# Sixteen-head attentions with a float32 values' product on column halves of TensorE

## The chip, the cores and the metric

The kernel runs on one NeuronCore of a Trainium2 chip. A core has TensorE (PE, the matrix engine), VectorE (DVE), ScalarE (ACT), GpSimd (POOL) and SyncE (SP, which here only starts loads). Each engine takes its own instructions in order, and semaphores order the engines among themselves. SBUF is the on-chip memory of 128 partitions; PSUM is the memory into which TensorE writes, in 8 banks of 512 float32 values a partition. The metric is the device time in microseconds (us); lower is better.

## The reference, cut to what matters

Two transformer blocks over 256 positions of width 1024, all in float32. The second block has two attentions of 16 heads each. For every head a softmax of scores over 256 keys is multiplied with 64-wide values:

```python
def block_attention(q, k, v, scale):          # 8 + 8 heads: "att2" in the kernel
    sc = jnp.einsum('bkgqd,bksd->bkgqs', qblk, kt).astype(jnp.float32) * scale
    p = jax.nn.softmax(sc, axis=-1).astype(vt.dtype)
    return jnp.einsum('bkgqs,bksd->bkgqd', p, vt)

def neighbourhood_attention(h, w_qkv, rpb, w_out):   # 16 heads: "att3"
    sc = jnp.einsum('bhqd,bhqkd->bhqk', qblk, kg).astype(jnp.float32) * scale + bias[None]
    p = jax.nn.softmax(sc, axis=-1).astype(vg.dtype)
    return jnp.einsum('bhqk,bhqkd->bhqd', p, vg)
```

The rest (a first block with convolutions and a 4-head attention "att1", and three feed-forward layers) is not touched.

## The kernel before, in words

Nearly every product is made in three passes: each operand is split into an upper part in fp32r (a reduced-precision float32 that TensorE multiplies in one pass) and the lower rest, and upper x upper, upper x lower and lower x upper are summed in PSUM. ScalarE makes the upper parts (`..hi`), VectorE or GpSimd the lower ones (`..lo`). The weights come in 1 MB groups through three slots (`raw`, `whi`, `wlo`), and the output projection of an attention is woven into its heads, so that the weights' work hides behind them.

The order of the work is written out by hand: each engine's block of code calls the same steps in its own order. No scheduler and no planner is involved. In att2 and att3 the 16 heads are 8 pairs (`PAIRS`). The steps of a head i of pair u, with the names used from here on:

- S(u), scores: TensorE, `pair_scores` or `scores` (lines 2209 and 2159). They go to PSUM bank 0 (even head) and 1 (odd head). Where a head's queries and keys take 64 partitions (pairs 0 to 3 of att2, all of att3), the products of the two heads stand on the two row halves of the array (64x128); pairs 4 to 7 of att2 take 96 rows and use the whole array.
- maxima: VectorE (line 1290; in att3 line 1283, two instructions a head that also add the bias).
- exp(i), exponentials: ScalarE (line 759), in place in the PSUM bank, with the row sums.
- divided(i): VectorE (lines 1299 and 1303), from that bank into `prob` in SBUF, 3 buffers.
- T(i), transposes of the probabilities: TensorE (line 2221), four 128x128, into the rows' bank. `rows_bank` gives bank 2 to all heads but head 1, which has bank 5 in att2 and bank 4 in att3.
- rows, split: ScalarE copies the bank into the upper part (line 802), VectorE makes the lower part (line 1310) and thereby frees the bank.
- V(i), values' product: TensorE, `head_times_values`, 6 products a head of 128x128 by 256 columns (line 2159, via `parts_product`). The values of a head are 64 wide; the other 64 columns of the left operand are zeros, so that both heads of a pair add up in bank 3. The values are split by GpSimd (`values_of`, lines 511 and 475), the zeros are written by ScalarE (`zeros_beside_values`, line 740).
- output, split: ScalarE (line 785) and VectorE (line 1339), out of bank 3.
- half(u, n): TensorE, half n of the output projection of pair u, 6 products of 512 columns (line 2013).

In round u of the loop in TensorE's `woven_heads` stand, for u of 3 and more: T(2u), V(2u-1), S(u+1), half(u-2, 1), T(2u+1), V(2u), half(u-1, 0). The first pairs of scores and T(0) are issued ahead of the loop. The scores of pair u+1 wait for `at_p`, that is for divided() of pair u, since exponentials and division both use the scores' banks.

## Time and profile before

| | us |
|---|---|
| median of 3 runs (1154.97 to 1155.78) | 1155.02 |
| the profiled execution, its own time | 1157.38 |
| its span | 1155.6 |
| TensorE (PE) busy | 1140.1 (99%) |
| VectorE busy | 839.0 (73%) |
| ScalarE busy | 628.1 (54%) |
| GpSimd busy | 497.3 (43%) |
| the woven heads of att2 in the span | about 621 to 672 |
| the woven heads of att3 in the span | about 921 to 972 |

The span is what the profile's rows cover; the profiled execution's own time also counts what lies around it. Busy time of an engine is the union of its instructions. A matmul's row shows its full duration, from the first column to the last result, while the next one may start long before it ends: the distance between two starts is the cost of a matmul, and the duration is not. The granted TensorE clock is at full speed (the mean is 0.998) throughout.

### The profile page before, as it was taken

What the parts mean: (1) busy time and instruction counts of PE and PEld (TensorE: products, weight loads), DVE (VectorE), ACT (ScalarE), POOL (GpSimd) and SP (SyncE); (2) the same over time, 40 slices, a digit from 0 to 9 for tenths busy, and PEclk for the clock granted to TensorE, in tenths of its full rate; (3) what the DMA queues carried; (4) which work ended last, traced back from release to release, by engine and by line L of the source; (5) the groups of instructions that cost most, each with busy time, mean ns of one, the idle gap of its engine ahead of it and who ended that gap; (6) DMA issues with size and microseconds to landing.
All of it is one profiled execution on the core that took longest, in us unless ns stands there. A gap on an engine that the chain in (4) does not pass through costs nothing.

```text
span 1155.6 us, 18538 instructions
## 1 busy us (share of the span) xinstructions
PE 1140.1 (99%) x6964; PEld 1019.0 (88%) x6964; DVE 839.0 (73%) x1100; ACT 628.1 (54%) x858; POOL 497.3 (43%) x433
## 2 busy tenths in 40 slices
PE   8999999999999999999999999999999999999997
PEld 8999999889998888888897888888888888888886
DVE  4687989886676898777898776665666676656655
ACT  6544433566644666555668755444464677444443
POOL 2699998897200633333233528880010455000000
PEclk9999999999999999999999999999999999999999
DMA  9555555563357456545442287556555513665651
GB/s 301 181 183 184 182 182 182 182 217 110 114 179 221 155 198 198 200 163 195 156 138 106 74 230 252 182 185 207 189 171 194 177 42 120 208 193 192 197 181 37
DMA packets 142809, 201.08 MB, mean 174 GB/s; under 512 B 3300, under 2 KB 123108, under 8 KB 142748
## 3 DMA queue, kind: packets, MB, share of 16 engines
q1 hardware_dynamic: 141776, 196.88, 51.8%
q0 software_dynamic: 912, 3.17, 1.2%
q8 instruction: 39, 0.64, 0.2%
q10 hardware_dynamic: 60, 0.20, 0.1%
q14 instruction: 22, 0.18, 0.0%
HBM read 199.20 MB, written 1.05 MB: 173 GB/s over the span
## 4 chain that ended last, share of the span: by engine, by line
PE 91%; DVE 2%; issue 2%; POOL 2%; ACT 2%; DMA 0%; POOLq 0%; ACTq 0%; DVEq 0%
PE ps L2013 52%; PE ps L2050 21%; PE ps L2055 11%; PE ps L2159 3%; PE ps L2221 1%; POOL wlo L483 1%; PE ps L2209 1%; PE ps L2141 1%; POOL merged L598 0%; DMA x<-in_x 0%; DVE work L1303 0%; PE ps L2127 0%; ACT ps L759 0%; DVE p_parts L1235 0%; PE ps L2427 0%
## 5 line engine op out<-in xcount | busy, mean ns | idle before, releaser
L1208 DVE TENSOR_TENSOR wlo<-raw,whi 128x2048 fp32r<-128x2048 f32 (+1 forms) x162 | 376.7, 2326 | 130.8 <-ACT whi L669 129.8
L669 ACT ACTIVATE whi<-raw 128x2048 fp32r<-128x2048 f32 (+1 forms) x178 | 337.4, 1897 | 140.9 <-PE ps L2013 134.4
L2050 PE MATMUL ps<-p_parts,whi 128*128 128x512 f32 x1184 | 289.3, 391 | 0.0
L2050 PEld LDWEIGHTS ps<-p_parts,whi 128*128 128x128 f32 x1184 | 220.1, 188 | 44.8
L2013 PE MATMUL ps<-p_parts,whi 128*128 128x256 f32 x912 | 166.4, 285 | 0.6 <-DVE p_parts L1235 0.6
L2055 PE MATMUL ps<-p_parts,wlo 128*128 128x256 f32 x1184 | 163.3, 282 | 0.0
L2055 PEld LDWEIGHTS ps<-p_parts,wlo 128*128 128x128 f32 x1184 | 155.8, 191 | 5.5
L2013 PE MATMUL ps<-whi,q_hi 128*128 128x512 f32 x380 | 148.6, 391 | 0.2 <-POOL wlo L483 0.2
L2013 PE MATMUL ps<-whi,q_lo 128*128 128x512 f32 x380 | 148.3, 390 | 0.0
L2013 PE MATMUL ps<-wlo,q_hi 128*128 128x512 f32 x380 | 147.9, 389 | 0.0
L2013 PEld LDWEIGHTS ps<-p_parts,whi 128*128 128x128 f32 x912 | 143.7, 194 | 1.1 <-issue 1.0
L483 POOL TENSOR_TENSOR wlo<-raw,whi 128x512 fp32r<-128x512 f32 x60 | 83.4, 1415 | 108.0 <-ACT whi L669 98.8
L2013 PE MATMUL ps<-p_parts,wlo 128*128 128x256 f32 x456 | 129.7, 284 | 0.0
L573 POOL TENSOR_SCALAR work<-misc,vec 128x256 f32<-128x256 f32 x84 | 125.2, 1490 | 0.0
L469 POOL TENSOR_TENSOR stat<-stat 128x1 f32<-128x1 f32 x14 | 10.0, 745 | 223.7 <-DVE stat L1216 210.6
L876 ACT ACTIVATE work<-ps 128x512 f32<-128x512 f32 x52 | 30.9, 595 | 135.1 <-PE ps L2055 135.0
L577 POOL TENSOR_TENSOR misc<-misc,work 128x256 f32<-128x256 f32 x84 | 91.5, 1090 | 7.0
L2013 PEld LDWEIGHTS ps<-p_parts,wlo 128*128 128x128 f32 x456 | 88.3, 194 | 0.0
L2013 PEld LDWEIGHTS ps<-wlo,q_hi 128*128 128x128 f32 x380 | 71.4, 188 | 15.2
L2013 PEld LDWEIGHTS ps<-whi,q_hi 128*128 128x128 f32 x380 | 71.5, 188 | 14.3 <-issue 0.5
L2013 PEld LDWEIGHTS ps<-whi,q_lo 128*128 128x128 f32 x380 | 71.5, 188 | 13.2
L491 POOL TENSOR_TENSOR wlo<-raw,whi 128x2048 fp32r<-128x2048 f32 x5 | 23.6, 4725 | 101.9 <-ACT whi L669 101.9
(320 smaller groups left out, 1835.6 us busy)
## 6 DMA issues: line engine op xcount, KB each, us to landing
raw<-in_w_in SPq DMA_DIRECT2D x35, 1024.0 KB, 5.0
raw<-in_w_up SPq DMA_DIRECT2D x22, 1024.0 KB, 5.1
raw<-in_up_a SPq DMA_DIRECT2D x16, 1024.0 KB, 5.4
raw<-in_down_a SPq DMA_DIRECT2D x16, 1024.0 KB, 4.9
raw<-in_up_b SPq DMA_DIRECT2D x16, 1024.0 KB, 5.4
raw<-in_down_b SPq DMA_DIRECT2D x16, 1024.0 KB, 4.9
raw<-in_od_w_qkv SPq DMA_DIRECT2D x12, 1024.0 KB, 5.1
raw<-in_w_down SPq DMA_DIRECT2D x11, 1024.0 KB, 5.0
```

The costliest lines, as they stand in the source:

```text
L483: last = nc.gpsimd.tensor_tensor(out=wlo[:, g % R, part], in0=raw[:, g % R, part], in1=whi[:, g % R, part].bitcast(F32), op=ALU.subtract)
L491: nc.gpsimd.tensor_tensor(out=wlo[:, g % R, :], in0=raw[:, g % R, :], in1=whi[:, g % R, :].bitcast(F32), op=ALU.subtract).then_inc(lo_read ...
L573: nc.gpsimd.tensor_scalar(tap, src, w, None, ALU.mult).then_inc(pool_mul, 1)
L577: nc.gpsimd.tensor_tensor(out=dst, in0=dst, in1=tap, op=ALU.add).then_inc(pool_tap, 1)
L669: nc.scalar.activation(whi[:, g % R, 0:n], raw[:, g % R, 0:n], ACT.Copy).then_inc(hi_ready, 1)
L876: return nc.scalar.activation(dst.rearrange("p (h n) -> p h n", h=2), ps[:, 2 * pb:2 * pb + 2, S:BW], ACT.Copy)
L1208: nc.vector.tensor_tensor(wlo[:, g % R, 0:n], raw[:, g % R, 0:n], whi[:, g % R, 0:n].bitcast(F32), ALU.subtract).then_inc(lo_ready[g % R], 1)
L2013: ins = nc.tensor.matmul(dst, lhs, rhs, start=first and n == 0, stop=last and n == 2)
L2050: return nc.tensor.matmul(bank(2 * pb + h), whi[:, r, at], p_parts[:, :, S * k:S * k + S], start=k == 0, stop=False)
L2055: return nc.tensor.matmul(bank(2 * pb + h, 0, S), wlo[:, r, at], p_hi[:, S * k:S * k + S], start=False, stop=k == KD - 1)
L2141: last = nc.tensor.transpose(bank(low + c // 2, c % 2 * S + P * t, c % 2 * S + P * t + P), x[:, t, P * c:P * c + P], ident[:, :])
L2159: ins = nc.tensor.matmul(dst, a, b, start=first and n == 0, stop=last and n == 2)
```

## The change

The change concerns att2 and att3; of att1 only the place of its maxima in `stat` moves.

1. The values' product is one float32 product with the unsplit operands: for each pair 2 heads x 2 halves of the keys, 4 matmuls of 128x64 by 256 columns. The even head's result is written to partitions 0 to 63 and the odd one's to 64 to 127 of bank 3, so the left operands stand on the two column halves of the array (the built program has tile size 128x64 for them). The zeros beside the values, the split of the values on GpSimd, and the split of the transposed rows are gone. A transposed row block is copied out once, into one of four SBUF buffers (`turned_rows`): by ScalarE for even heads, by VectorE for odd ones.
2. Exponentials are written to four SBUF buffers (`exp_rows`); in att3 the biased scores go there as well. A score bank is therefore free once the exponentials are done (att2) or once the maxima with the bias are done (att3), and the division reads SBUF.
3. Scores run two pairs ahead instead of one: in round u the order on TensorE is T(2u), V of pair u-1, T(2u+1), S(u+2), half(u-2, 1), half(u-1, 0). ScalarE's and VectorE's loops are written in a matching new order.

```diff
+        turned_rows = [misc[:, 1024 + 512 * n:1536 + 512 * n] for n in range(4)]
+        exp_rows = [a.rearrange("p (t n) -> p t n", t=T) for a in (work[:, 0:512], work[:, 2048:2560],
+                                                                   misc[:, 3072:3584], misc[:, 3584:4096])]
...
             def exponentials(name, i):
                 units, H, u0, n0, biased, k = ATT[name]
                 act.wait_ge(at_nm, n0 + i + 1)
+                if name != "att1" and i >= 4:
+                    act.wait_ge(at_p, n0 + i - 3)
                 for t in range(T):
                     scored = bank(S_BANK[name] + i % 2, t * S, t * S + S)
-                    src = bsc[:, i % 2, t, :] if biased else scored
-                    last = nc.scalar.activation(scored, src, ACT.Exp,
-                                                bias=att_nmax[:, 2 * (i % 2) + t:2 * (i % 2) + t + 1],
+                    dst = scored if name == "att1" else exp_rows[i % 4][:, t, :]
+                    last = nc.scalar.activation(dst, dst if biased else scored, ACT.Exp,
+                                                bias=att_nmax[:, 2 * (i % 4) + t:2 * (i % 4) + t + 1],
...
-                def rows_upper(i):
+                def rows_out(i):
                     act.wait_ge(at_t, n0 + i + 1)
-                    if i >= 2:
-                        act.wait_ge(at_v, n0 + i - 1)
-                    nc.scalar.activation(unit_hi[i % 2][:, PT], bank(rows_bank(name, i)[0]), ACT.Copy).then_inc(at_h, 1)
+                    if i >= 4:
+                        act.wait_ge(at_v, n0 + i - 3)
+                    b = rows_bank(name, i)[0]
+                    nc.scalar.activation(turned_rows[i % 4], bank(b), ACT.Copy).then_inc(bank_read[b], 1)
...
-                    if u == 1:
-                        rows_upper(2 * u + 1)
-                    if u + 1 < PAIRS and u:
-                        exponentials(name, 2 * u + 2)
-                    if u != 1:
-                        rows_upper(2 * u + 1)
-                    if u + 1 < PAIRS and u:
-                        exponentials(name, 2 * u + 3)
...
                         queries_keys(name, u + 3)
+                    if u + 2 < PAIRS:
+                        exponentials(name, 2 * u + 4)
+                        exponentials(name, 2 * u + 5)
...
-                nc.vector.tensor_tensor(prob[:, i % 3], ps[:, S_BANK[name] + i % 2, :].rearrange("p (t n) -> p t n", t=T),
-                                        inv.to_broadcast([P, T, S]), ALU.mult).then_inc(at_p, 1)
+                rows = ps[:, S_BANK[name] + i % 2, :].rearrange("p (t n) -> p t n", t=T) if name == "att1" else exp_rows[i % 4]
+                nc.vector.tensor_tensor(prob[:, i % 3], rows, inv.to_broadcast([P, T, S]), ALU.mult).then_inc(at_p, 1)
...
+                    rows_out(2 * u + 1)
+                    if u:
+                        output_lower(u - 1)
+                    if u + 2 < PAIRS:
+                        maxima(name, 2 * u + 4)
+                        maxima(name, 2 * u + 5)
...
                 if u:
-                    pe.wait_ge(at_p, n0 + 2 * u)
+                    pe.wait_ge(at_nm if biased else at_e, n0 + 2 * u)
...
+                def pair_times_values(u):
...
+                    for i in (2 * u, 2 * u + 1):
+                        b, uses = rows_bank(name, i)
+                        free(b, uses + 1)
                     free(3, USES[name][3] + u)
                     for m in range(2):
-                        v0, p0 = UNIT_V + S * m + HD * h, UNIT + S * m
-                        ins = parts_product(bank(3, 0, S), [a[:, v0:v0 + P] for a in unit_sides(u, H)],
-                                            [a[i % 2][:, p0:p0 + S] for a in (unit_hi, unit_lo)],
-                                            h == 0 and m == 0, h == 1 and m == 1)
-                    ins.then_inc(at_v, 1)
+                        for h in range(2):
+                            rows = turned_rows[(2 * u + h) % 4]
+                            ins = nc.tensor.matmul(ps[HD * h:HD * h + HD, 3, 0:S], units[u]["v"][:, m, h, :], rows[:, S * m:S * m + S],
+                                                   start=m == 0, stop=m == 1)
+                            if m == 1:
+                                ins.then_inc(at_v, 1)
...
                 for u in range(PAIRS + 1):
...
+                    if 0 < u < PAIRS:
                         rows_transposed(name, 2 * u, *rows_bank(name, 2 * u))
...
+                    if u:
+                        pair_times_values(u - 1)
                     if u < PAIRS:
                         rows_transposed(name, 2 * u + 1, *rows_bank(name, 2 * u + 1))
-                        head_times_values(2 * u)
+                    if u + 2 < PAIRS:
+                        pair_scores(name, u + 2)
+                    if u > 1:
+                        half_of_output(u - 2, 1)
                     if u:
                         half_of_output(u - 1, 0)
```

How the order changes is shown at three places; the line numbers of the changed kernel differ from those of the one before. First TensorE in att2 of the kernel before, from T(1) on (`x3` counts equal instructions in a row, the brackets name the semaphores waited for; L2221 transposes, L2159 values' product, L2209 scores):

```order
L2221 MATMUL ps<-ident,work 128x128 [waits at_p,bank_read5]
L2221 MATMUL ps<-ident,work 128x128 x3
L2159 MATMUL ps<-q_hi 128x256 [waits bank_read2,bank_read3,v_lo,v_zero]
...
L2221 MATMUL ps<-ident,work 128x128 [waits at_p,bank_read2]
L2221 MATMUL ps<-ident,work 128x128 x3
L2159 MATMUL ps<-p_parts,q_hi 128x256 [waits bank_read3,bank_read5,v_lo]
...
L2209 MATMUL ps<-p_parts,q_hi 128x256 [waits at_p,qk_lo]
...
L2221 MATMUL ps<-ident,work 128x128 [waits at_p,bank_read2]
L2221 MATMUL ps<-ident,work 128x128 x3
```

The same place of TensorE in the changed kernel (L2178 transposes, L2218 values' product, L2166 scores):

```order
L2178 MATMUL ps<-ident,work 128x128 [waits at_p,bank_read5]
L2178 MATMUL ps<-ident,work 128x128 x3
L2166 MATMUL ps<-p_parts,q_hi 128x256 [waits at_e,qk_lo]
...
L2178 MATMUL ps<-ident,work 128x128 [waits at_p,bank_read2]
L2178 MATMUL ps<-ident,work 128x128 x3
L2218 MATMUL ps<-misc,gates 64x256 [waits bank_read5,bank_read2,bank_read3,bank_read7]
L2218 MATMUL ps<-misc,gates 64x256 x3
L2178 MATMUL ps<-ident,work 128x128 [waits at_p,bank_read2]
L2178 MATMUL ps<-ident,work 128x128 x3
L2166 MATMUL ps<-p_parts 128x256 [waits at_e,qk_lo]
```

S(2) now stands ahead of T(2) and of every values' product, V(0) and V(1) are one block behind T(2), and S(3) follows T(3) directly; S waits for exponentials (`at_e`) instead of a division (`at_p`).

ScalarE in att2 of the changed kernel, from the exponentials of heads 2 and 3 on (L728 exponentials, L716 half of a weight group's upper part, L695 queries or keys, L774 rows copied out, L754 output):

```order
L728 ACTIVATE misc,stat<-ps,stat 128x256 [waits at_nm]
L728 ACTIVATE misc,stat<-ps,stat 128x256
L716 ACTIVATE whi<-raw 128x1024 [waits slot_used,raw_in2]
L695 ACTIVATE p_parts<-merged 128x256 [waits at_s,bank_read6]
L728 ACTIVATE work,stat<-ps,stat 128x256 [waits at_p,at_nm]
L728 ACTIVATE work,stat<-ps,stat 128x256
L728 ACTIVATE work,stat<-ps,stat 128x256 [waits at_p,at_nm]
L728 ACTIVATE work,stat<-ps,stat 128x256
L774 ACTIVATE misc<-ps 128x512 [waits at_t]
L754 ACTIVATE o_up<-ps 128x256 [waits at_v]
```

And of the kernel before, from the same exponentials on (L759 exponentials, L802 rows' upper part, L722 queries or keys, L749 weights, L785 output):

```order
L759 ACTIVATE ps,stat<-ps,stat 128x256 [waits at_nm]
L759 ACTIVATE ps,stat<-ps,stat 128x256
L802 ACTIVATE p_parts<-ps 128x512 [waits at_t]
L722 ACTIVATE q_hi<-merged 128x256 [waits at_s,at_q]
L749 ACTIVATE whi<-raw 128x1024 [waits slot_used,raw_in2]
L722 ACTIVATE p_parts<-merged 128x256 [waits at_s,bank_read6]
L802 ACTIVATE q_hi<-ps 128x512 [waits at_v,at_t]
L785 ACTIVATE o_up<-ps 128x256 [waits at_v]
```

The copy of the rows of head 2 (L774 now, L802 in the last but one row before) stood ahead of the exponentials of heads 4 and 5 and now stands behind them.

VectorE in att2 of the changed kernel, from the division of head 2 on (L1260 divided, L1305 copies of keys, L1320 rows of head 1 copied out, L1246 maxima of heads 4 and 5):

```order
L1260 TENSOR_TENSOR work<-misc,stat 128x512 [waits at_rs]
L1305 COPY vreg<-ps 96x512 [waits ev_tr]
L1255 RECIPROCAL stat<-stat 128x2 [waits at_e]
L1260 TENSOR_TENSOR work<-misc,stat 128x512 [waits at_t,at_rs]
L1305 COPY vreg<-ps 96x512 [waits ev_tr] x2
L1320 COPY misc<-ps 128x512 [waits at_t]
L1246 TENSOR_REDUCE stat<-ps 128x2 [waits at_s] x2
```

Before, the lower part of the rows of head 1 (L1310) stood ahead of the division of head 3:

```order
L1303 TENSOR_TENSOR work<-ps,stat 128x512 [waits at_rs]
L1354 COPY vreg<-ps 96x512 [waits ev_tr]
L1310 TENSOR_TENSOR p_parts<-ps,p_parts 128x512 [waits at_h]
L1299 RECIPROCAL stat<-stat 128x2 [waits at_e]
L1303 TENSOR_TENSOR work<-ps,stat 128x512 [waits at_t,at_rs]
L1354 COPY vreg<-ps 96x512 [waits ev_tr] x2
```

The rows of head 1, which the first values' product needs, now come behind one division and two more copies.

## Rows read from the trace of the kernel before

**Rows 1.** Windows: from:to, length, then busy us and instructions of each engine.

```profile
616.50:625.00 8.50, 7.75 (x68) 7.02 (x68) 8.43 (x14) 8.28 (x22) 1.46 (x2) 1.00 0.37 125
625.00:638.00 13.00, 11.43 (x82) 9.75 (x81) 9.07 (x20) 10.66 (x29) 9.03 (x8) 1.00 0.13 35
...
921.50:937.00 15.50, 14.35 (x111) 12.15 (x111) 10.99 (x33) 12.65 (x35) 7.47 (x13) 1.00 0.22 67
937.00:972.00 35.00, 35.00 (x234) 29.56 (x230) 24.36 (x70) 25.01 (x66) 24.41 (x26) 1.00 0.20 65
```

**Rows 2.** Waits of TensorE: line waited for, total us, times, longest.

```profile
PE ps L2221 <- DVE p_parts L1310: 1.6, 2, 0.8
```

**Rows 3.** Timeline of TensorE, end of att2: start, us, engine, line, what.

```profile
661.80 0.60 PE L2221 MATMUL ps<-ident,work 128*128 128x128 f32 x4
662.15 0.48 PE L2159 MATMUL ps<-p_parts,q_hi 128*128 128x256 f32 x2
662.47 0.28 PE L2159 MATMUL ps<-p_parts,q_lo 128*128 128x256 f32 x1
...
666.86 0.88 PE L2159 MATMUL ps<-p_parts 128*128 128x256 f32 x6
667.57 0.40 PE L2013 MATMUL ps<-whi,o_up 128*128 128x512 f32 x1
```

**Rows 4.** Timeline of TensorE: unsplit float32 products of the layer norm (L2414).

```profile
278.93 3.61 PE L2414 MATMUL ps<-misc,mean_w 128*128 128x256 f32 x16
282.38 0.60 PE L2221 MATMUL ps<-ident,work 128*128 128x128 f32 x4
```

**Rows 5.** Timeline of TensorE in att3: into and out of scores on row halves.

```profile
907.64 0.39 PE L2013 MATMUL ps<-wlo,p_parts 128*128 128x512 f32 x1
907.96 0.39 PE L2209 MATMUL ps<-q_hi 64*128 64x256 f32 x2
908.18 0.28 PE L2209 MATMUL ps<-q_lo,q_hi 64*128 64x256 f32 x2
...
925.14 0.28 PE L2209 MATMUL ps<-q_hi,q_lo 64*128 64x256 f32 x2
925.35 0.66 PE L2221 MATMUL ps<-ident,work 128*128 128x128 f32 x4
925.76 0.36 PE L2159 MATMUL ps<-q_hi,p_parts 128*128 128x256 f32 x1
```

**Rows 6.** Timeline of ScalarE, start of att2's loop.

```profile
619.70 0.47 ACT L759 ACTIVATE ps<-ps,stat 128x256 f32<-128x256 f32 x1
...
620.60 0.46 ACT L759 ACTIVATE ps<-ps,stat 128x256 f32<-128x256 f32 x1
...
622.28 1.09 ACT L749 ACTIVATE whi<-raw 128x1024 fp32r<-128x1024 f32 x1
623.23 0.45 ACT L722 ACTIVATE p_parts<-merged 128x256 fp32r<-128x256 f32 x1
```

**Rows 7.** Timeline of VectorE, start of att2's loop.

```profile
619.85 0.68 DVE L1354 COPY vreg<-ps 96x512 f32<-96x512 f32 x1
...
621.23 0.69 DVE L1303 TENSOR_TENSOR work<-ps,stat 128x512 f32<-128x512 f32 x1
621.84 0.68 DVE L1354 COPY vreg<-ps 96x512 f32<-96x512 f32 x1
...
625.95 1.28 DVE L1290 TENSOR_REDUCE stat<-ps 128x2 f32<-128x512 f32 x2
```

**Rows 8.** Timelines of TensorE and, for the second row, ScalarE in both loops.

```profile
638.25 0.40 PE L2013 MATMUL ps<-whi,o_up 128*128 128x512 f32 x1
...
920.62 0.47 ACT L759 ACTIVATE ps<-misc,stat 128x256 f32<-128x256 f32 x1
...
921.50 0.60 PE L2221 MATMUL ps<-ident,work 128*128 128x128 f32 x4
...
937.34 0.50 PE L2013 MATMUL ps<-whi,o_up 128*128 128x512 f32 x1
```

More of the change, by code:

```diff
@@ L315, in two_blocks, with values_in @@
         WEIGHTS_LO_DVE = {"att2": {11: G_EVO + 3, 15: G_F2A}, "att3": {}}
-        def shared_side(name, u):
-            return name == "att2" and u in (2, 3)
-        def values_ready(name, u):
-            return {"att1": u + 1, "att2": 5 + u - (1 if u == 2 else 2 if u > 2 else 0), "att3": 11 + u}[name]
+        def values_in(name, u):
+            if name == "att2":
+                return [(b, USES["ev_in"][b] + 1) for b in (5, 7)] if u == 0 else [(b, USES["ukv"][b] + 1) for b in range(4, 8)]
+            return [(b, USES["v"][b] + 1) for b in ((4, 6) if u == 0 else (5, 7))]
         def unit_sides(u, H):
@@ L533, in woven_heads @@
                     queries_keys(2)
-                    values(0)
-                    values(1)
                 for i in range(HEADS):
                     u = i // 2
-                    if i % 2 == 0 and 1 <= u < PAIRS - 1:
-                        values(u + 1)
                     if i % 2 and u + 3 < PAIRS:
@@ L612, in _ @@
             inverse_root("n_mix2a")
-            for b in (5, 7):
-                pool.wait_ge(bank_read[b], USES["ev_in"][b] + 1)
-            values_of("att2", 0)
             pool.wait_ge(h_ms, 1)
@@ L621, in _ @@
                                         in1=mhalf[:, 0:2], op=ALU.pow).then_inc(l_r, 1)
-                if part == 0:
-                    pool.wait_ge(slot_used, G_LAT + 3)
-                    values_of("att2", 1)
             woven_heads("att2")
@@ L735, in values @@
                 split_upper([unit_parts(u, units[u], H)[1]]).then_inc(v_hi, 1)
-            def zeros_beside_values(parts):
-                for part in parts:
-                    gap = part[:, UNIT_V:UNIT_V + T * 256].rearrange("p (t n) -> p t n", t=T)[:, :, HD:P]
-                    nc.scalar.activation(gap, ident[:, :].rearrange("p (t n) -> p t n", t=T), ACT.Copy,
-                                         scale=0.0).then_inc(v_zero, 1)
             def hi_half(g, n):
@@ L792, in woven_heads @@
                     latent_keys_values(1)
+                    act.wait_ge(at_q, 1)
+                    queries_keys(name, 2)
                     for n, (b, kind, c) in enumerate(B_FILLS[:4]):
@@ L1362, in woven_heads, with rows_out @@
                     lo(G_V + 4)
-                for u in range(PAIRS):
-                    rows_lower(name, 2 * u)
-                    if u:
-                        output_lower(u - 1)
-                    if u + 1 < PAIRS and not (u == 0 and name == "att2"):
-                        maxima(name, 2 * u + 2)
-                        maxima(name, 2 * u + 3)
+                def rows_out(i):
+                    dve.wait_ge(at_t, n0 + i + 1)
+                    if i >= 4:
+                        dve.wait_ge(at_v, n0 + i - 3)
+                    b = rows_bank(name, i)[0]
+                    nc.vector.tensor_copy(turned_rows[i % 4], bank(b)).then_inc(bank_read[b], 1)
+                for u in range(PAIRS):
                     if u == 0 and name == "att3":
+                        maxima(name, 2)
+                        maxima(name, 3)
                         lo(G_V + 5)
-                    if u == 1:
-                        rows_lower(name, 2 * u + 1)
                     if u + 1 < PAIRS:
```

75 lines of the change are left out of this document (14 added, 61 removed).

## The prediction

> **What bounds the kernel now.** I read the windows first. In the settled part of att3, 937 to 972, TensorE is busy for 35.00 of 35.00 us, and no other engine over 26; the idle time lies at the starts of the two loops of woven heads: 0.75 us in 616.5 to 625, 1.57 in 625 to 638, 1.15 in 921.5 to 937 [rows 1]. So TensorE is the bound, and the change can act in two ways only: through the cost of what TensorE issues, and through the 3.5 us of waits. The list of waits then says for what it waits there: mainly, T for the lower part of the rows, which frees the rows' bank [rows 2]. Third comes TensorE's timeline, in which the distance from start to start is the price. Relief of VectorE, ScalarE and GpSimd is worth nothing by itself.
>
> **The values' product.** Before, 6 products take 667.57 - 666.86 = 0.71 us (0.118 each), so a pair's 12 take 1.42; the first after transposes comes 0.08 late (0.32 for two products against 0.24), twice a pair: 1.58 us [rows 3]. Now there are 4 unsplit float32 products of 256 columns. The trace has such a product over the full array: 8 of them leave 16 records and take 282.38 - 278.93 = 3.45 us, so 0.431 a product and 0.216 a record, two records (with a weight load each) a product [rows 4]. No row shows a float32 product on a column half, or two column halves at once. The row halves do run side by side: two products start every 0.12 us (908.18 after 907.96 is late only by the switch) [rows 5]. The ends are 4 x 0.431 = 1.72 us, nothing side by side, and 2 x 0.431 = 0.86, all of it. I take the value between them that the order of the records gives: they start in order, and go left, left, right, right. The second left record must wait for the first, the first right one can run beside the second left one, and so on: 5 slots of 0.216, 1.08 us.
>
> To this comes the change of tiling. For the row halves, the way in costs 0.09 (907.96 instead of 907.64 + 0.23) and 0.10 (0.22 to the next pair instead of 0.12); the way out into transposes costs 0.09 (925.35 instead of 925.26) and 0.06 (transposes of 0.41 instead of 0.35) [rows 3, 5]. I take the same 0.34 for the column halves; the ends are 0 and 0.68. A pair now costs 1.42. Then the scores stand behind transposes instead of behind V: 0.08 to 0.10 more. Per pair 1.08 + 0.34 + 0.09 - 1.58 = -0.07; over 16 pairs -1.1 us.
>
> The Trainium skill, TensorEngine Tiling (Array Packing), Key Properties, says that a change of the tiling mode drains TensorE while a change of tile within a mode doesn't. The trace agrees, with 0.34 us for a stay on row halves. By that rule every V pays it, as in the sum above; without it the sum would be 16 x 0.34 = 5.4 us lower.
>
> **The start of att2's loop.** I walk it on the clock of before. Nothing ahead of it changes on TensorE; queries for pair 2 now come before the wait for transposes and cost ScalarE nothing. Durations: a head's exponentials 0.90, half a weight group 0.95, rows copied by ScalarE 0.5 [rows 6]; a VectorE step of 512 columns 0.61, maxima of two heads 1.28, a division with its reciprocal 0.80 [rows 7]; T 0.35 [rows 3]; a half of the output projection 6 x 0.23 = 1.39; S on row halves 6 x 0.12 and the switches, 0.9 [rows 3, 5].
> - S(2) now waits for the exponentials of head 3, which start at 620.60: S(2) at 621.75, T(2) at 622.65, over at 623.0.
> - V of pair 0 needs the rows of head 1 from VectorE. That does division 2 (to 621.6), one copy (622.2), division 3 (623.0), two copies (624.2), and only then the rows: 624.9. V waits 1.9 us and runs to 626.2.
> - T(3) needs the bank that ScalarE's copy of the rows of head 2 frees. ScalarE's order has the exponentials of heads 4 and 5 ahead of it, whose maxima VectorE makes behind the rows of head 1: 625.45, exponentials to 627.3, rows 627.85. T(3) at 627.95, 1.7 us late.
> - S(3) to 629.3; half(0,0) waits 0.4 for the output's lower part, now behind two divisions and the rows of head 3: done 631.1. T(4), V(1) to 632.8; T(5) waits until 633.65 for the rows of head 4, behind the exponentials of 6 and 7 and half a weight group on ScalarE. S(4), two halves: 638.3.
> Before, at 638.25, the same scores and three halves of output are done, and one more T and one more pair of V [rows 8]. These cost 0.35 + 1.5, so the changed kernel is 1.85 us behind. All waits of before are paid in this already.
>
> **The start of att3's loop.** The same walk: T(1) at 921.50 [rows 8], S(2) to 922.85 (it waits only for maxima), T(2), V of pair 0 to 924.6; exponentials of head 3 end about 921.1 [rows 8]; VectorE then has division 3, the rows of head 1 (922.75), and four maxima steps, about 1.4 us (924.55); exponentials of 4 and 5 to 925.75, rows of head 2 to 926.3. T(3) at 926.35, 1.7 us late; S(3), half(0,0) from 928.05; T(5) late by 0.9; three halves done at 936.4. With the missing T and V: 938.2, against 937.34 before [rows 8]. Cost 0.9 us.
>
> **The settled rounds.** From S(u+2) to T(2u+3): maxima and exponentials take 0.8 + 1.9 = 2.7 us, the copy of rows ends at about 3.9 behind T(2u+2); TensorE gets there after two halves, T and V, at 4.4. 0.5 us of slack. In att3, VectorE starts the maxima some 0.4 late (rows and output come first while S is short), and where ScalarE also makes half a weight group (0.95) ahead of the rows, T is late by 0.35 or so. That is three or so rounds: 1.0 us. In att2 the scores of 96 rows are longer (1.42) and cover it. The removed zeros and splits are hidden by TensorE's work: 0.
>
> **The sum.** -1.1 + 1.85 + 0.9 + 1.0 = +2.6 us. The profiled execution would take 1157.38 + 2.6 = 1160.0 (span 1158.2 and 1.8 around it); it stands 2.36 above the median of the runs shown, so the median is 1155.02 + 2.6 = 1157.6.
>
> **Rivals.**
> - The lead does its work, and the kernel is faster. Place: T(3), T(5) and V of pair 0 in both loops. If the copies out come in time (as they do if ScalarE and VectorE reach them before the exponentials, which rounds of settled work with 0.5 us of slack speak for, and the two orders above against), the 3.5 us of waits go and none come: -1.1 - 3.5 = -4.6, 1150.4. It decides from a copy of rows less than 0.4 us after TensorE is ready. 25%.
> - The column halves don't run side by side. V is 1.72 + 0.34: 0.64 x 16 = 10.3 us more; four of these V lie in waits that the start has anyway (-2.6), and the late T of the settled rounds are gone (-1.0): +9.3, 1164.3. For it: no row has two streams from the same 128 partitions. Against: the row halves [rows 5]. 20%.
> - The halves overlap in full, V 0.86. 0.22 x 16 = 3.5 less, but the starts and the T that wait for ScalarE take back 1.3 of it: +0.4, 1155.4. 8%. The Trainium skill (TensorE: Matmul & The Clock Gate, The mechanism) has tiles of one array start about 4 ns apart while matmuls keep their order. By the first half of that V would cost 0.86, by the second the left pair's second record holds back the right one, as in my 1.08.
>
> **How the numbers follow.** Forecast, some waits traded for others: 47%, own range 1155.5 to 1160 (walks of 1 us error each, a switch from 0 to 0.68). This measurement can tell about 0.2%, 2.3 us, from no change; the forecast lies just above this bound, and I give slower 28 of its 47, same 19. With the serial halves slower has 48 in all. Faster takes the 25 of the first rival and 2 of the full overlap: 27; same has 19 and the other 6 of the full overlap: 25. The range reaches from the faster rival to the serial halves: 1150 to 1165.
>
> **What would show it.** Right: the eight records of a pair's values' product start at five times, 0.216 us apart, with a gap of some 0.2 us ahead of them; waits of T for ScalarE's copy (1.7 us in each loop) and one of V for VectorE's copy of 1.9 us in att2; TensorE's idle in 616.5 to 640 some 5 us or more. Wrong: records of left and right at one start (0.86) or all 0.216 apart with no overlap (1.72); a window without idle at the starts of the loops; or scores that wait for exponentials in settled rounds, which I don't expect.

## The result: slower, 1160.44 us against 1155.02

Six runs of the changed kernel have a median of 1160.44 us (1159.87 to 1161.43), six of the kernel before 1155.02: a ratio of 1.0040, 95% interval 1.0029 to 1.0050. The forecast was 1157.6, slower, with a range of 1150 to 1165. Of the runs told below, one of lead_one's twelve took 2462.24 us and is left out of its median; one_side ran once.

The profiled execution took 1160.57 us (span 1158.8, TensorE 98% busy), 3.19 more than that of before. I measured the stages on TensorE's timeline, from the first row of S(0) to the first transposes of the sum behind the attention, since the untouched stages in front ran 1.6 us faster in this execution than in the one of before.

| us | before | changed |
|---|---|---|
| att2, S(0) to its end | 61.53 | 65.91 |
| att3, S(0) to its end | 62.09 | 62.21 |
| a settled round of att2, T(2u) to T(2u+2) | 6.54 | 6.24 |
| a settled round of att3 | 6.24 | 5.89 |

So the settled rounds became cheaper, and the loops' starts ate more than that. The windows of the changed kernel, columns as in [rows 1] (length; busy us and count of PE, PEld, DVE, ACT, POOL; granted clock; DMA share, GB/s):

```profile
616.50:621.50 5.00, 4.62 (x45) 4.03 (x42) 4.93 (x8) 4.79 (x14) 0.23 (x2) 1.00 0.29 79
621.50:625.00 3.50, 1.33 (x11) 0.58 (x9) 3.04 (x6) 1.02 (x5) 0.64 (x1) 0.96 0.47 191
625.00:627.30 2.30, 0.85 (x4) 0.71 (x4) 1.72 (x4) 2.30 (x7) 0.00 (x0) 0.50 0.00 0
627.30:631.30 4.00, 4.00 (x19) 3.17 (x18) 2.61 (x6) 2.73 (x10) 3.61 (x3) 0.50 0.01 2
631.30:638.00 6.70, 6.25 (x39) 4.61 (x38) 6.67 (x7) 3.66 (x9) 6.70 (x6) 0.98 0.16 37
923.00:930.00 7.00, 5.14 (x41) 3.62 (x41) 5.23 (x17) 4.97 (x18) 1.52 (x2) 1.00 0.49 150
930.00:941.00 11.00, 9.65 (x70) 6.93 (x68) 8.12 (x28) 8.93 (x26) 3.16 (x5) 1.00 0.01 1
```

From 616.5 to 638 TensorE is idle for 4.45 us (2.32 in [rows 1]), and from 625 to 631.3 it runs at a granted clock of 0.50, 1.2 GHz, which happens nowhere in these stages of before. Its timeline there (start, us, engine, line, what; in brackets the idle time ahead and what ended it):

```profile
621.09 0.66 PE L2178 MATMUL ps<-ident,work 128*128 128x128 f32 x4
623.60 1.08 PE L2218 MATMUL ps<-misc,gates 128*64 128x256 f32 x8 [1.85 <-DVE misc L1320]
626.45 1.11 PE L2178 MATMUL ps<-ident,work 128*128 128x128 f32 x4 [1.77 <-ACT misc L774]
627.50 1.65 PE L2166 MATMUL ps<-p_parts 64*128 64x256 f32 x12
629.07 0.79 PE L1970 MATMUL ps<-whi,o_up 128*128 128x512 f32 x1
...
630.09 0.63 PE L1970 MATMUL ps<-wlo,o_up 128*128 128x512 f32 x1
630.52 0.63 PE L1970 MATMUL ps<-whi,o_up 128*128 128x512 f32 x1
...
631.71 0.49 PE L2178 MATMUL ps<-ident,work 128*128 128x128 f32 x3
```

V of pair 0 waits 1.85 us for VectorE's copy of rows, T(3) 1.77 for ScalarE's. Behind that a product of 512 columns starts every 0.43 us instead of every 0.23, and T(3), S(3) and half(0,0) take 5.26 us. The waits of TensorE over the whole span (line waited for: total us, times, longest), where [rows 2] had 1.6 us for T:

```profile
PE ps L2178 <- ACT misc L774: 5.8, 5, 1.9
...
PE ps L2218 <- DVE misc L1320: 1.9, 1, 1.9
PE ps L1970 <- DVE o_low L1290: 1.6, 3, 0.9
```

The values' product in a settled round, where [rows 3] had 0.71 for one head's six products:

```profile
645.85 0.60 PE L2178 MATMUL ps<-ident,work 128*128 128x128 f32 x4
646.38 1.08 PE L2218 MATMUL ps<-misc,gates 128*64 128x256 f32 x8
647.39 0.66 PE L2178 MATMUL ps<-ident,work 128*128 128x128 f32 x4
```

Windows of 0.05 us show its eight records starting two at a time, at 646.38, 646.64, 646.86 and 647.07: four steps, not five. Last, VectorE and GpSimd behind the start of att2:

```profile
631.16 3.30 DVE L1260 TENSOR_TENSOR work<-misc,stat 128x512 f32<-128x512 f32 x1
634.39 0.15 DVE L1255 RECIPROCAL stat<-stat 128x2 f32<-128x2 f32 x1
634.58 1.59 DVE L1260 TENSOR_TENSOR work<-misc,stat 128x512 f32<-128x512 f32 x1
```

```profile
630.16 1.28 POOL L475 TENSOR_TENSOR q_lo<-kreg,q_hi 96x512 fp32r<-96x512 f32 x1
631.40 1.28 POOL L475 TENSOR_TENSOR q_lo<-vreg,q_hi 96x512 fp32r<-96x512 f32 x1
632.64 2.99 POOL L483 TENSOR_TENSOR wlo<-raw,whi 128x512 fp32r<-128x512 f32 x2
635.58 1.72 POOL L475 TENSOR_TENSOR p_parts<-kreg,p_parts 96x512 fp32r<-96x512 f32 x1
```

Two divisions take 3.30 and 1.59 us; from PSUM the same division took 0.69 [rows 7]. The longer one, from 631.16 to 634.46, stands beside four of GpSimd's instructions.

### The profile page after: what moved, and what is told of

It is laid out like the page before. It is cut to its first block, busy times and chain, and to the rows that moved or that the text cites. A ratio compares the mean times of both kernels' runs of the same rounds, so it can differ in the third digit from the quotient of the medians.

```text
span 1158.8 us, 18344 instructions
## 1 busy us (share of the span) xinstructions
PE 1136.5 (98%) x6900; PEld 1004.2 (87%) x6900; DVE 835.1 (72%) x1084; ACT 618.5 (53%) x834; POOL 484.0 (42%) x405
## 3 DMA queue, kind: packets, MB, share of 16 engines
HBM read 199.20 MB, written 1.05 MB: 173 GB/s over the span
## 4 chain that ended last, share of the span: by engine, by line
PE 92%; DVE 3%; ACT 2%; issue 2%; POOL 0%; DMA 0%; POOLq 0%; DVEq 0%; ACTq 0%
PE ps L1970 51%; PE ps L2007 23%; PE ps L2012 12%; PE ps L2116 1%; PE ps L2178 1%; PE ps L2218 1%; PE ps L2098 1%; PE ps L2166 1%; ACT work L728 0%; DVE work L1260 0%; DMA x<-in_x 0%; DVE misc L1320 0%; DVE stat L1246 0%; PE ps L2084 0%; ACT misc L728 0%
```

## The theories and the experiments

My theory: (a) the copies of rows come late by the fixed orders of ScalarE and VectorE; (b) these waits let TensorE's clock fall, some 2.3 us in att2; (c) divisions that read SBUF are held up by GpSimd, some 1.4 us; (d) the values' product itself is cheaper. The rivals: the chain from scores to division sets the start whatever the order; the low clock costs nothing, since the steps behind it wait for other engines anyway; and the column halves with their switch are no cheaper. All edits are to the changed kernel. The results together, medians beside the kernel before on the same chip, and att2 and att3 in us from the profiled execution, one for each row (the changed kernel: ratio 1.0040, 1.0029 to 1.0050; 65.91 and 62.21):

| run | us (before) | ratio, interval | att2 | att3 |
|---|---|---|---|---|
| v_by_head | 1160.75 (1154.95) | 1.0050, 1.0037 to 1.0064 | 65.98 | 62.85 |
| one_side | 1168.24 (1155.04), one run | | 69.31 | 66.93 |
| fill | 1162.09 (1154.95) | 1.0056, 1.0042 to 1.0069 | 66.73 | 63.33 |
| fill_ahead | 1159.60 (1155.04) | 1.0034, 1.0021 to 1.0047 | 65.83 | 62.29 |
| pool_thin | 1159.20 (1154.95) | 1.0034, 1.0021 to 1.0048 | 64.38 | 62.24 |
| exp_psum | 1158.39 (1155.04) | 1.0028, 1.0019 to 1.0037 | 64.91 | 62.56 |
| copies_first | 1159.59 (1154.95) | 1.0039, 1.0025 to 1.0053 | 64.69 | 63.10 |
| lead_one | 1157.00 (1155.04) | 1.0019, 1.0009 to 1.0029 | 63.05 | 62.14 |
| one_v_only | 1153.20 (1155.85) | 0.9977, 0.9967 to 0.9987 | 59.61 | 61.75 |
| two_reordered | 1161.60 (1155.85) | 1.0055, 1.0037 to 1.0073 | 65.97 | 62.61 |
| two_mended | 1155.10 (1155.15) | 0.9997, 0.9986 to 1.0008 | 64.11 | 59.76 |
| two_final | 1151.89 (1155.12) | 0.9963, 0.9950 to 0.9975 | 59.62 | 59.07 |

The intervals of the six full rows from v_by_head to copies_first overlap that of the changed kernel. What these runs show is therefore read from their traces, one execution each, and not from their totals. two_reordered's overlaps it and lead_one's touches it too; those of one_v_only, two_mended and two_final lie clearly below.

### How the column halves overlap: v_by_head and one_side

```diff
-                    for m in range(2):
-                        for h in range(2):
+                    for h in range(2):
+                        for m in range(2):
```

> Changed kernel with the four products of a pair of values in another order: both products of the left column half, then both of the right one, instead of by turns. Theory that the order left, left, right, right of records runs two at a time because the next product always goes to the other half: in the new order the two products of a half can't overlap each other, only the second record of the left half's last product can lie beside the first of the right: 7 slots of 0.216 instead of 4, 1.51 us a pair instead of 0.86, 16 x 0.65 = 10.4 more, less some 2 of them that lie in waits: 1168 to 1171. Rival (the chip reorders freely between the halves, or a product over a column half takes half the time anyway): 1160.4, starts as before.

No change: the records still start two at a time, four steps. Either the halves overlap whatever the order, or a product on 64 columns takes half the time by itself. The second run keeps this order and puts both heads on one half:

```diff
-   nc.tensor.matmul(ps[HD * h:HD * h + HD, 3, 0:S], ...
+   nc.tensor.matmul(ps[0:HD, 3, S * h:S * h + S], ...
```

> Changed kernel, in which both heads of a pair take their product of values in the left column half (the second into the next 256 columns of the bank), head by head; the right half of the output's rows isn't computed. Theory A (left and right run side by side, and the chip lets the right half's records run ahead of queued left ones): with one half alone nothing can overlap, 8 records start 0.216 us apart, 1.72 us a pair, 16 x 0.86 = 13.8 more less 2 to 3 in the starts' waits, 1171 to 1173. Theory B (the two records of one float32 product with 64 columns run at the same time, whichever half it is in, so that a product takes 0.216 and the two halves don't overlap at all): the starts stay two at a time, 0.22 to 0.26 apart, 1160 to 1161.

TensorE's timeline, first v_by_head, then one_side:

```profile
645.71 1.09 PE L2218 MATMUL ps<-misc,gates 128*64 128x256 f32 x8
646.73 0.66 PE L2178 MATMUL ps<-ident,work 128*128 128x128 f32 x4
```

```profile
645.81 1.94 PE L2218 MATMUL ps<-misc,gates 128*64 128x256 f32 x8
647.68 0.66 PE L2178 MATMUL ps<-ident,work 128*128 128x128 f32 x4
```

On one half the product takes 1.87 us to the next T instead of 1.02, 0.85 more, which is four records of 0.216. So the two halves do run side by side, and a right record doesn't stand behind a queued left one. My theory for v_by_head is refuted, theory A of the second run holds in the trace. The whole time rose by 7.8 us and not by 11 to 13: a slower V fills the waits of the starts. TensorE's listed waits in the heads fall from 6.0 to 3.4 us in att2 and from 3.6 to 1.5 in att3.

### The clock: fill and fill_ahead

Idle transposes of the identity on TensorE, as `fill` placed them (behind V's waits, so its first 20 came too late and pushed V back), and as `fill_ahead` did. The edit shown is that of fill_ahead, cut to its first 16 transposes; 14 more stand ahead of T(3):

```diff
                 def pair_times_values(u):
+                    if name == "att2" and u == 0:
+                        free(3, USES[name][3])
+                        for n in range(16):
+                            nc.tensor.transpose(bank(3, P * (n % 4), P * (n % 4) + P), ident[:, :], ident[:, :])
```

> Changed kernel with 20 transposes of the identity (0.088 us each, 1.76 us) on TensorE ahead of V of pair 0 and 18 more (1.6 us) ahead of T(3), in att2 alone, inside the two waits. They compute nothing that is used. Theory that the waits let TensorE's clock fall, and that the fall costs 2.3 us: the granted clock stays near 1.00 in 625 to 631, T(3) takes 0.35, S(3) about 1.3 and half(0,0) 1.4 us, and the time is 2.3 us lower, 1158.1 (up to 0.3 more where the fill overshoots). Rival (the lower clock has another cause, a power or a fixed moment, or the late steps are bound by others anyway): 1160.4 to 1161.

> Changed kernel with transposes of the identity on TensorE inside the two waits at att2's start: 16 ahead of V of pair 0's waits (0.11 us each as the trace of the earlier run shows, 1.8 us) and 14 ahead of T(3) (1.6 us), none of them behind a wait. They compute nothing that is used. Theory that idle time lets the clock fall: V of pair 0 and T(3) start when they did, the granted clock stays at 1.00 in 625 to 631, T(3), S(3) and half(0,0) take 3.3 us instead of 5.3, and att2's stage is 63.9 instead of 65.9 us: 1158.4. Rival (the later steps wait for other engines anyway): 0.5 us or less, 1160.

TensorE's timeline in fill:

```profile
623.01 2.38 PE L2217 MATMUL ps<-ident 128*128 128x128 f32 x20 [1.85 <-DVE misc L1320]
...
628.35 0.60 PE L2178 MATMUL ps<-ident,work 128*128 128x128 f32 x4
...
630.15 0.47 PE L1970 MATMUL ps<-whi,o_up 128*128 128x512 f32 x1 [0.30 <-DVE o_low L1290]
630.46 0.39 PE L1970 MATMUL ps<-whi,o_low 128*128 128x512 f32 x1
...
631.62 0.60 PE L2178 MATMUL ps<-ident,work 128*128 128x128 f32 x4
```

With work in the second wait the granted clock is 1.00 from 625 to 631.3, and T(3), S(3) and half(0,0) take 3.27 us (628.35 to 631.62) instead of 5.26, a wait of 0.30 included: the lower clock cost 2.0 us here. The totals don't show it, and my expectation of the total failed twice. fill spent the gain on V's delay. fill_ahead kept the clock up there too and reached T(4) 21.3 us behind S(0) instead of 23.2, but T(7) no earlier than the changed kernel (32.5 us behind S(0) instead of 32.6): in between T(5) waits 0.82 us for rows and S(4) 0.77 for GpSimd's queries, and behind these waits the clock falls to 0.54, in 637 to 640. att2 stayed at 65.83. So the mechanism was right and the total went by the rival: the steps behind wait for others anyway. Here filling moved the fall and didn't avoid it. What each fall costs over all runs is not separated from their spread.

### Divisions beside GpSimd: pool_thin and exp_psum

```diff
-   part = slice(BW * n, BW * n + BW)        # pool_thin, GpSimd's weights in att2
+   part = slice(BW * n, BW * n + 8)
-   dst = scored if name == "att1" else exp_rows[i % 4][:, t, :]      # exp_psum
+   dst = exp_rows[i % 4][:, t, :] if name == "att3" else scored
```

> Changed kernel, in which GpSimd's eight lower parts of output weights within att2 are 8 columns wide instead of 512; the rest of these lower parts is left out, so GpSimd works some 12 us less between 627 and 652. Theory that divisions which read SBUF are held up by GpSimd's work on SBUF: the divisions of 3.30 and 1.59 us take 0.69, the rows of head 5, the output's lower part and T(7) come in time, and the time is about 1.4 us lower, 1159.0. If the queries' and keys' lower parts (96 x 512, which stay) alone are what holds VectorE, half of that: 1159.7. Rival (the two long divisions have another cause, or cost TensorE nothing because the lower clock sets the pace there): 1160.4.

> Changed kernel, in which att2's exponentials are written over the scores in PSUM as before, so that the divisions read PSUM, and the scores of the next pair wait for the divisions instead of the exponentials; att3 as changed. Theory that divisions from SBUF are held up by GpSimd: all divisions of att2 take 0.69 us, the waits of T(7) (0.83) and half(1,0) (0.45) go, 1.3 us less; against that S(2) waits some 1.3 us for the division of head 3, most of which comes out of the wait of 1.85 behind it. 1159.2. Rival (no contention; the tighter wait costs): 1161.

(pool_thin's lines stand in a copy of the function that att2 alone uses.) With less work on GpSimd (12.9 us busy in 627 to 652 instead of 21.1) the longest division is 1.12 us instead of 3.30, the waits of half(1,0) and T(7) are gone, and att2 is 1.53 us shorter (1.4 expected). exp_psum gained 1.0 in att2 and lost the same two waits, in spite of a new wait of 1.63 us of S(2) and of the lower clock from 621.5 to 631. Its median is 2 us lower, 1158.39 (1159.2 expected). The clearest rows are those of one_v_only below, whose exponentials are in PSUM: all divisions of att2, against those of the changed kernel in the second fence (count: minimum/median/maximum ns). exp_psum's sixteen divisions of att2 read the same, 691/692/692.

```profile
L1260 DVE TENSOR_TENSOR work<-ps,stat x16: 690/692/692, 611.1 to 656.5; 128x512 f32<-128x512 f32 x16
```

```profile
L1260 DVE TENSOR_TENSOR work<-work,stat x8: 691/694/1118, 612.2 to 652.8; 128x512 f32<-128x512 f32 x8
L1260 DVE TENSOR_TENSOR work<-misc,stat x8: 692/731/3304, 619.5 to 661.0; 128x512 f32<-128x512 f32 x8
```

Same instruction, GpSimd as busy (26.4 us in 608 to 670, 24.4 in the changed kernel), one operand in PSUM instead of SBUF: none above 0.692 us. Most divisions from SBUF take 0.69 as well; a few are held up for long. The Trainium skill, SBUF — State Buffer, SBUF: two separate sides, states that VectorE with two SBUF inputs and a GpSimd instruction that reads SBUF take turns on one pair of ports, and that the loser fully blocks. The traces agree, with 3.30 us beside GpSimd and 0.692 at most from PSUM; that ports are the cause no row shows directly. The prediction gave the division's new operand no price at all.

### The order of the copies: copies_first

```diff
+                    if u == 0:
+                        rows_out(2)
                     if u + 2 < PAIRS:
                         exponentials(name, 2 * u + 4)
```

(and on VectorE the rows of head 1 ahead of the division of head 3, and the last two latent keys behind the maxima.)

> Changed kernel, with the copies of rows put earlier at the start of both loops: ScalarE copies the rows of head 2 ahead of the exponentials of heads 4 and 5, VectorE copies the rows of head 1 ahead of the division of head 3, and in att2 the last two latent keys come after the maxima. My theory (fixed orders on ScalarE and VectorE make V of pair 0 and T(3) late, and the idle time lets TensorE's clock fall): the 1.85 us ahead of V of pair 0 in att2 and the 1.77 and 1.85 us ahead of T(3) go; S(3) of att2 then waits some 1.6 us for the exponentials of head 5; the clock stays at its upper level behind that (2.3 us back). In sum -2.0 in att2's start, -2.3 of clock, -1.6 in att3: about 1154.5 us. Rival (the chain S, maxima, exponentials sets the start whatever the order of the copies, and the clock falls all the same): the waits move to S(3) and half(0,0), 1159 to 1160.5 us.

The waits for rows ahead of V of pair 0 and of both T(3) went, as said. In their place stood 1.93 us of S(3) (1.6 expected) and, not expected, 1.39 us in att2 and 2.30 in att3 of half(0,0) for the output's lower part, which VectorE makes behind two divisions. The clock fell all the same (0.67 in 627.3 to 631.3, 0.66 in 930 to 935), and the time was 1159.59, not 1154.5. The rival was right for this edit: moving one step of a chain shows the next.

### Undoing parts: lead_one and one_v_only

Of lead_one only TensorE's part is shown:

```diff
+                    if 0 < u < PAIRS - 1:
+                        pair_scores(name, u + 1)
                     if u < PAIRS:
                         rows_transposed(name, 2 * u + 1, ...)
-                    if u + 2 < PAIRS:
-                        pair_scores(name, u + 2)
```

> Changed kernel with the scores one pair ahead as before: S(u+1) stands ahead of T(2u+1), maxima, exponentials and divisions stand in the rounds that they had before; the values' product on column halves, the exponentials in SBUF and the shared copies of rows stay. Theory (the values' product is cheaper by about 0.38 us a pair, 16 x 0.38 = 6 us, and all of it and more is lost to the waits that the lead of two pairs brings at the loops' starts): the waits of 1.85, 1.77, 1.85 and 1.05 us go, the clock stays at its upper level, att2 takes 58.5 to 59.5 us, att3 59 to 60, and the time is 1149 to 1151. Rival (the column halves themselves, with their change of tiling, are no cheaper than before, and the lead is worth something): 1155 to 1158.

> Changed kernel with two parts undone: scores one pair ahead, and exponentials in PSUM as before (the divisions read PSUM), in both attentions; the orders of the second round as before (half(0,1) ahead of T(4), rows of head 3 ahead of the division of head 4). What stays of the change is the values' product on column halves and the shared copies of rows. Theory (each settled round of before is 6.54 us in att2 and 6.25 in att3, and with one pair ahead and the new product 6.38 and 6.10 as the earlier run showed; divisions of 1.12 and 4.23 us came from reading SBUF beside GpSimd): no wait above 0.7 us, no division above 0.75 us, att2 59.5 to 60, att3 60 to 60.5: 1151 to 1152. Rival (VectorE's long steps come from GpSimd whatever they read): 1156 to 1157 as the run before with SBUF.

lead_one missed its 1149 to 1151 and lies in the rival's 1155 to 1158. A wait of 1.89 us of T(4) stands in its trace, with a granted clock of 0.59 in 628 to 632 behind it, and a division of 4.23 us beside GpSimd. one_v_only, which also undoes the exponentials in SBUF and goes back to the second round's order of the kernel before, came out at 1153.2, 0.23% below the kernel before (1151 to 1152 expected; it has waits of 1.41 and 1.55 us that I had held below 0.7). Its settled rounds are 6.32 and 6.10 us, 0.22 and 0.14 below those of before; over 8 rounds each that is 2.9 us, and the medians differ by 2.65. This shows (d) for the product together with its shared copies of rows, which weren't tried apart, and that the loss came from the other parts together. It refutes the rival that the column halves are no cheaper.

### The orders worked out anew: two_reordered, two_mended, two_final

Scores two pairs ahead, in three steps. The core of the first edit (ScalarE) and, as the last line, of the second:

```diff
+                    if u < 2:
+                        rows_out(2 * u + 2)
                     if u + 2 < PAIRS:
                         exponentials(name, 2 * u + 4)
+                    if u < 2:
+                        output_upper(u)
...
+   dst = scored if name == "att1" or name == "att2" and i >= 6 else exp_rows[i % 4][:, t, :]
```

> Changed kernel (scores two pairs ahead, exponentials in SBUF) with the orders of the first two rounds of each loop worked out anew: ScalarE copies the rows of heads 2 and 4 ahead of the exponentials of the next pair and takes the output's upper part between the two heads' exponentials; VectorE copies the rows of heads 1 and 3 earlier and makes the maxima ahead of the division of head 3, the output's lower part right behind them; in att2 ScalarE takes the last two latent keys, GpSimd the queries of pair 4 ahead of the weights, and TensorE half(0,1) ahead of S(4). Theory (what the lead costs is nothing but these orders, at the starts, and the clock that falls in the waits): the idle time of att2's start falls from 3.6 us to about 1 and of att3's from 3.2 to below 0.5, the clock stays up, settled rounds keep 6.24 and 5.9 us; att2 60, att3 59 us: 1151. Rival (the chain scores, maxima, exponentials, division is too long for two pairs' lead at the start, whatever the order; the waits move to S(3), S(4) and the halves): 1156 to 1158.

> The reordered kernel with the scores two pairs ahead, with three more edits. In att2 the exponentials from head 6 on stay in PSUM (the divisions that run while GpSimd works read PSUM, and the scores from pair 4 on wait for divisions instead of exponentials), and the scores from pair 4 on stand behind a half of the output. In att3 ScalarE copies the values of the second half a round earlier, and the rows ahead of the weights' upper parts. Theory (the two long steps of VectorE, 1.72 and 4.04 us, cost the 3.11 and 0.97 us of waits of the earlier run, and the values and the weights those of 1.86 and 1.87): no division above 0.75 us in att2 from head 6 on, no wait above 0.9 us, att2 60 us, att3 59.5 us, 1151 to 1152, at or below the kernel with one pair ahead and the exponentials in PSUM (1153.2). Rival (a lead of two pairs leaves too little time between scores, division and the next scores once the divisions free PSUM): waits of S for VectorE from S(5) on, 1154 to 1157.

> The kernel of the run before (scores two pairs ahead) with three edits: in att2 VectorE takes both halves of the lower part of G_EVO+3's weights in round 6, behind the divisions, rows and output of that round, instead of the first in round 5, where it waited 3.63 us for ScalarE; ScalarE takes the output's upper part at the end of its round, ahead of the weights; in att3 the rows of head 6 are copied between the exponentials of heads 8 and 9. Theory: the wait of 3.46 us of half(5,0), the lower clock behind it (1 us) and the wait of 1.14 us in att3 go, nothing takes their place; att2 59.5, att3 58.7 us, and the time is 1149.5, 0.5% below before and clearly below the kernel with one pair ahead (1153.2). Rival (the later weights come too late for half(6,0), or another queue stands behind the moved steps): 1152 to 1155.

In two_reordered att2 went as planned up to 632: waits of 0.81 and 0.42 us, clock 1.00. Then VectorE:

```profile
628.95 1.72 DVE L1271 TENSOR_TENSOR work<-misc,stat 128x512 f32<-128x512 f32 x1
630.59 0.15 DVE L1266 RECIPROCAL stat<-stat 128x2 f32<-128x2 f32 x1
630.78 4.04 DVE L1271 TENSOR_TENSOR work<-misc,stat 128x512 f32<-128x512 f32 x1
```

and T(6) waited 3.11 us, T(7) 0.97, with a clock of 0.60 in 635.5 to 639.5. In att3 half(0,0) waited 1.86 us for ScalarE's copy of values and T(7) 1.87 for rows. The run took 1161.60, where I had said 1151 and the rival 1156 to 1158: new orders alone, with the divisions reading SBUF, are no better than the changed kernel's. With the divisions of att2 from head 6 on in PSUM (two_mended) both waits of att2 went, but one further back appeared, since VectorE's lower part of a weight group stood ahead of the divisions of round 6:

```profile
654.38 1.23 DVE L1289 TENSOR_TENSOR wlo<-raw,whi 128x1024 fp32r<-128x1024 f32 x1 [3.63 <-ACT whi L716]
```

half(5,0) waited 3.46 us for it, which missed my expectation for att2 by 4 us and that of the total by 3 to 4 (1155.10, in the rival's range but not by its waits); att3 came at 59.76 as expected. two_final moves that step; its waits on TensorE within the two stages are 0.78 us or less. Windows as in [rows 1]:

```profile
616.50:625.00 8.50, 7.34 (x64) 6.01 (x64) 8.43 (x13) 8.01 (x25) 1.45 (x2) 1.00 0.34 125
625.00:638.00 13.00, 12.23 (x82) 9.54 (x83) 8.57 (x19) 11.12 (x34) 8.77 (x8) 1.00 0.01 2
638.00:674.00 36.00, 35.43 (x211) 27.22 (x210) 25.09 (x46) 23.37 (x58) 17.13 (x12) 1.00 0.37 118
921.50:937.00 15.50, 15.12 (x109) 10.76 (x108) 12.52 (x45) 12.77 (x40) 5.89 (x7) 1.00 0.10 34
937.00:972.00 35.00, 34.89 (x211) 26.09 (x210) 20.52 (x61) 23.53 (x57) 22.65 (x17) 1.00 0.36 112
```

att2 takes 59.62 and att3 59.07 us, as expected to 0.4, and the time is 1151.89, 0.37% below the kernel before and about 0.75% below the changed one. I had said 1149.5; its six runs go from 1149.93 to 1153.15, and the place of att2's S(0), behind stages that no edit touches, differs between the executions of all runs by about as much (607.4 to 611.0). Its median is the lowest of all, but its interval overlaps that of one_v_only (0.9967 to 0.9987), so which of the two is faster is not shown. It does show that with the lead of two pairs the starts need not cost what they did: the rival that the chain sets the start whatever the order doesn't hold.

## Why the prediction was right, and where it wasn't

The direction, the place and the main waits were right. The total came out 2.8 us too low, and that it is so near is in part luck, the rest of larger errors of both signs: set against the terms of the sum, the product came out 4 us cheaper, att2's start 4.9 us dearer, and att3's start and rounds together 1.0 dearer. The other 0.9 lies behind the two stages (0.3) or is not placed (0.6).

- **What bounds.** TensorE, and nothing else: right. What of the difference can be placed is a wait, the clock or the product on TensorE.
- **The values' product, -1.1.** Too small by 4. The switches were right: 0.18 on the way in (0.53 less 0.35 for T) and 0.15 on the way out (1.01 less 0.86), 0.33 against 0.34. The term that failed is "5 slots of 0.216, 1.08 us": it is four, 0.86, and a pair costs 1.19 instead of 1.42. By the forecast's own sum that is -0.29 a pair; the settled rounds show -0.30 and -0.35, 16 pairs about -5. I had given this 8%, as a rival, because I took the order of the records for their order in time; one_side and v_by_head show that it isn't: between the two halves the matmuls don't keep the order in which they are issued, on which my 1.08 rested.
- **The start of att2, +1.85.** The walk held: V of pair 0 waits 1.85 (1.9 said), T(3) 1.77 (1.7). What it lacked: the clock, 2.0 to 2.3 us (5.26 - 3.27 in the runs with and without filling), the blocked divisions, from which T(7)'s 0.83 and half(1,0)'s 0.45 come (both are gone in pool_thin and exp_psum), and a wait of 0.89 for the output's lower part near the loop's end. The stage is 4.38 longer: -2.4 for eight cheaper rounds, +4.15 of waits (6.04 less 1.89), +2.3 of clock make 4.05; 0.3 stays open. Two more waits of the walk, 0.4 for half(0,0) and 0.85 for T(5), are missing in the changed kernel, whose TensorE comes to these steps late at half clock; with the clock up, in fill, they are there, 0.30 and 0.82. So as an estimate the lower clock made the stage longer by 2.3 - 1.1 = 1.2 us only.
- **The start of att3, +0.9.** T(3) waits 1.85 (1.7 said), T(5) 1.05 (0.9), half(0,0) 0.30: right. But a cheaper product in a round that waits for VectorE or ScalarE only lengthens the wait: att3's waits are 3.55 us against 1.15, which eats 2.4 of the 2.8 that its eight rounds give. The stage is 0.12 longer; 0.5 stays open.
- **The settled rounds, +1.0.** Nearly nothing: one T waits 0.35 in att3, where three or so were said.
- **"The removed zeros and splits are hidden: 0".** Nothing contradicts it; it wasn't tried by itself. But the same sentence should have priced the divisions' new place, and it didn't.
- **The rivals.** "The lead does its work", at 1150.4, is what two_final nearly reaches (1151.9) with other orders and most of att2's exponentials in PSUM; as the change orders them the copies come late in both loops, which is what the walk had said against it. The serial halves are refuted.

The stages give +4.5, with 0.3 behind them +4.8 of the 5.4 between the medians. The profiled execution is not one of the worst: in those of v_by_head, fill, exp_psum and copies_first the clock fell in att3 as well (0.66 to 0.77 in 930 to 935), which may be the rest. That is argued, not shown.

## What to carry to other kernels

Price a longer lead at the loop's first rounds, where no earlier work covers the steps, by walking each engine's own order; and expect that TensorE's clock may fall behind a wait of almost 2 us: here two waits of 3.62 us together were followed by 2.3 us of slower work, part of which came out of later waits. Moving an operand from PSUM to SBUF is an edit with a cost of its own if another engine works on SBUF then (GpSimd here): look at the longest instance of a group, not at its mean. When a change of several parts loses, undo them one at a time before giving up the one that pays.

## What the hardware showed that I had not expected

- Float32 products on two column halves start two at a time, 0.216 us a step, in either order of issue; on one half alone they take 0.85 us more a pair.
- TensorE's granted clock fell to 0.50 (1.2 GHz) behind waits of 1.85 and 1.77 us with 1.08 us of products between them, and stayed there for some 6 us. Single waits of 1.63 (exp_psum), 1.88 (one_side), 1.89 (lead_one), 3.11 (two_reordered) and 3.46 us (two_mended) were followed by it as well, and in fill_ahead waits of 0.82 and 0.77 us within 2.5. In att3 a wait of 1.85 us was followed by it in some executions (v_by_head, fill) and not in others (the changed kernel, pool_thin). Waits of 1.41 and 1.55 us (one_v_only) and of 1.86 and 1.87 (two_reordered, att3) left it at 1.00, and so did those of before, 0.84 us at most, and of two_final, 0.78 at most.
- A VectorE division of 0.69 us took up to 4.23 with both operands in SBUF beside GpSimd, and 0.692 at most with one in PSUM.
